# Turning x and the residual sum before they are normed, and squares summed on VectorE, in a one-core decoder trunk of two layers

## The reference

```
h = rms_norm(x, g)            # x * rsqrt(mean(x*x) + 1e-6) * g, over a row
# layer A: 16 heads of 64
q, k, v, gate = split(h @ w_in_a, 4)
x = x + (silu(gate) * stick_breaking(q, k, v)) @ w_out_a
# keys and values, shared: 8 heads, k = 2 components of 64, v = 128 wide
k, v = split(rms_norm(x, kv_norm_g) @ w_kv, 2)
k = rope(rms_norm(k, k_norm_g))
# layer B
q, gate = split(rms_norm(x, b_norm_g) @ w_in_b, 2)
q = rope(rms_norm(q, q_norm_g))
o = (softmax(q1 k1'/8) - lam * softmax(q2 k2'/8)) v       # causal
o = rms_norm(o, subln_g) * (1 - lam_init)
x = x + (silu(gate) * o) @ w_out_b
```

## Time and profile before

| | us |
|---|---|
| runs | 641.98, 640.73, 641.54 |
| median | 641.54 |
| profiled execution, its own time | 644.41 |
| span of that execution | 643.1 |
| TensorE busy | 620.0 (96%) |
| VectorE busy | 452.9 (70%) |
| ScalarE busy | 349.6 (54%) |
| GpSimd busy | 351.2 (55%) |
| chain that ended last, by engine | PE 65%, DVE 21%, ACT 7% |

### The profile page before, as it was taken

How to read it: one execution, slowest core, us unless ns; L and a number is a source line. 1 busy time by engine, 2 the same in 40 slices (tenths; PEclk the granted TensorE clock), 3 DMA queues, 4 the chain that set the end, 5 groups by cost and what they waited for, 6 DMA issues and landing times.

```text
span 643.1 us, 9970 instructions
## 1 busy us (share of the span) xinstructions
PE 620.0 (96%) x3260; PEld 522.0 (81%) x3260; DVE 452.9 (70%) x717; ACT 349.6 (54%) x764; POOL 351.2 (55%) x335
## 2 busy tenths in 40 slices
PE   5899999999999999999989999999899999999998
PEld 4788887888888888878878888788687888887786
DVE  3476168989889898884146398426789999998531
ACT  5342284967869678684336544325356645576320
POOL 4557448547576475735342545457564676556161
PEclk9999998999999999999999999999899999999999
DMA  7433313112121121212121322230421220221142
GB/s 261 104 97 95 93 35 99 49 51 65 45 86 49 49 65 49 82 34 66 66 66 43 106 93 88 82 107 25 123 74 50 82 82 12 70 83 65 34 133 97
DMA packets 61774, 49.09 MB, mean 76 GB/s; under 512 B 7728, under 2 KB 48816, under 8 KB 61744
## 3 DMA queue, kind: packets, MB, share of 16 engines
q1 hardware_dynamic: 58064, 48.25, 24.4%
q10 hardware_dynamic: 3680, 0.46, 0.5%
HBM read 44.50 MB, written 2.10 MB: 72 GB/s over the span
## 4 chain that ended last, share of the span: by engine, by line
PE 65%; DVE 21%; ACT 7%; issue 4%; DMA 1%; SPq 0%; DVEq 0%; POOL 0%; ACTq 0%
PE bank L607 17%; PE bank L609 17%; PE bank L608 17%; PE bank L730 4%; ACT pr L1366 4%; PE bank L744 3%; PE bank L706 3%; DVE small L1749 1%; DVE pr L1770 1%; DVE lo L1561 1%; DVE h_hi L1494 1%; DVE lo L1539 1%; DVE v L1446 1%; DVE at_lo L1804 1%; DMA xs<-in_x 1%
## 5 line engine op out<-in xcount | busy, mean ns | idle before, releaser
L484 POOL TENSOR_TENSOR w_lo<-w_raw,w_hi 128x512 fp32r<-128x512 f32 x64 | 87.0, 1367 | 123.6 <-ACT w_hi L1045 123.6
L496 POOL TENSOR_TENSOR w_lo<-w_raw,w_hi 128x512 fp32r<-128x512 f32 x96 | 139.0, 1448 | 7.7
L494 POOL CAST w_hi<-w_raw 128x512 fp32r<-128x512 f32 x96 | 74.6, 777 | 120.7 <-DVE pr L1770 38.2
L607 PE MATMUL bank<-h_hi,w_hi 128*128 128x512 f32 x320 | 129.4, 404 | 2.8 <-ACT q L1275 2.7
L607 PE MATMUL bank<-w_hi,h_hi 128*128 128x512 f32 x320 | 128.6, 402 | 2.9 <-DVE h_lo L1452 2.8
L609 PE MATMUL bank<-w_hi,h_lo 128*128 128x512 f32 x320 | 126.1, 394 | 0.0
L608 PE MATMUL bank<-w_lo,h_hi 128*128 128x512 f32 x320 | 125.8, 393 | 0.0
L609 PE MATMUL bank<-h_hi,w_lo 128*128 128x512 f32 x320 | 125.5, 392 | 0.0
L608 PE MATMUL bank<-h_lo,w_hi 128*128 128x512 f32 x320 | 125.2, 391 | 0.0
L1045 ACT ACTIVATE w_hi<-w_raw 128x512 fp32r<-128x512 f32 x64 | 39.6, 628 | 65.0 <-PE bank L609 64.9
L607 PEld LDWEIGHTS bank<-h_hi,w_hi 128*128 128x128 f32 x320 | 60.1, 188 | 17.2 <-issue 2.2
(11 more groups left out here) (183 smaller groups left out, 1202.2 us busy)
## 6 DMA issues: line engine op xcount, KB each, us to landing
w_raw<-in_a_w_in SPq DMA_DIRECT2D x64, 256.0 KB, 2.7
w_raw<-in_w_kv SPq DMA_DIRECT2D x32, 256.0 KB, 3.0
w_raw<-in_b_w_in SPq DMA_DIRECT2D x32, 256.0 KB, 2.8
w_raw<-in_a_w_out SPq DMA_DIRECT2D x16, 256.0 KB, 2.8
w_raw<-in_b_w_out SPq DMA_DIRECT2D x16, 256.0 KB, 3.0
xs<-in_x SPq DMA_DIRECT2D x4, 512.0 KB, 4.8
qrot<-qs SPq DMA_DIRECT2D x32, 64.0 KB, 2.0
out_x<-xs SPq DMA_DIRECT2D x8, 256.0 KB, 2.7
```

The costliest lines, as they stand in the source:

```text
L484: nc.gpsimd.tensor_tensor(w_lo[s][:, :], w_raw[s][:, :], w_hi[s][:, :].bitcast(F32), ALU.subtract).then_inc(s_w, 1)
L494: nc.gpsimd.tensor_copy(w_hi[s][:, :], w_raw[s][:, :]).then_inc(s_whi, 1)
L496: nc.gpsimd.tensor_tensor(w_lo[s][:, :], w_raw[s][:, :], w_hi[s][:, :].bitcast(F32), ALU.subtract).then_inc(s_w, 1)
L607: pe.matmul(o, ahi, bhi, start=start, stop=False, skip_group_check=True)
```

## The change

Four things are written differently.

1. **Start.** TensorE transposes x itself, each of its four row blocks as it lands, with 4, 8, 4 and 8 `keep_busy` matmuls between. ScalarE and VectorE split the transposed x with the gain but without the root, into h2; the values' product runs on that, and the root is applied when the values are copied out (`scale=rx`). For q, k and gates the transposed x is copied raw, the roots are transposed too (`turn_roots`, four transposes), multiplied in by VectorE (`query_scale`) and split into h1 (`query_hi`, `query_lo`). Nine small parameters come by SyncE's queue between slabs. The rotary tables are built in one orientation and turned by eight transposes (`turn_tables`).
2. **Between the layers.** The same with the new stream: no `keep_busy`; tiles 0 to 3 are transposed inside the output product after its k=1 (`turn_sum(0)`), tiles 4 to 7 after the third step of the key/value product, with four transposes of the roots. Keys and values are scaled by the root as they are copied out. Banks are given by tables (`TURN_BANK`, `KV_BANK`).
3. **A head of layer B.** The squares are no longer summed on TensorE: they are transposed into banks 1 and 3 (`turned_squares`, eight transposes), and VectorE adds them there (`turned_means`, two `tensor_reduce`). `scores_b` of the next head, whose first matmuls write those banks, waits for it (s_rq). The root's logarithm and exponential stand one head later on ScalarE (`head_root` in `gate_parts`), and `at_lo` ahead of the means on VectorE. ScalarE takes over `keep_hi`, the hi part of two of each head's slabs and of the values; the copy of q stands before the last exponentials. GpSimd waits for the q rotation (s_qct) and for the roots (s_rb) before its splits, and the cosine product of `q_rotate` waits for q_lo.
4. **Last head.** ScalarE does two output slabs and the root of head 6 before the gate's logarithm.

```diff
+
+            tr = pe.transpose(bank[4 + k % 4][:, cols(t * P, P)], xs[:, t, cols(k * P, P)], ident[:, :])
+            if t == TT - 1:
+                tr.then_inc(s_tp, 1)
+
+        def turn_roots(n, o):
+
+            pe.wait_ge(s_rx, n + 1)
...
+                tr = pe.transpose(o[:, cols(t * P, P)], rx[:, t:t + 1].to_broadcast([P, P]), ident[:, :])
+            tr.then_inc(s_rt, 1)
...
-        keep_busy(neg_one[:, :], BUSY_A)
-        turn_input(0, 4, 0, 0)
+        for t in range(TT):
+            pe.wait_ge(s_x[t], 16)
+            for k in range(4):
+                turn_input(k, t)
+            keep_busy(neg_one[:, :], BUSY_A[t])
...
+                if half == 0 and k < 3:
+                    pe.wait_ge(s_raw, k + 1)
+                    for t in range(TT):
+                        turn_input(k + 4, t)
+                if half == 0 and k == 3:
+                    pe.wait_ge(s_raw, 4)
+                    turn_roots(0, bank[7])
+                if half == 0 and k == 4:
+                    pe.wait_ge(s_rc, 1)
+                    for t in range(TT):
+                        turn_input(7, t)
...
+        def turn_sum(half, tiles=range(TT)):
+
+            for k in (half * TT + n for n in tiles):
+                for t in range(TT):
+                    pe.wait_ge(s_x2, half * TT + t + 1)
+                    tr = pe.transpose(bank[TURN_BANK[k]][:, cols(t * P, P)], xs[:, t, cols(k * P, P)], ident[:, :])
+                tr.then_inc(s_tp, 1)
+
         for k in range(KT):
             bulk_step(G_OUT + KT + k, TT, k, h2_hi, h2_lo, banks_of=OUT_BANK_A)
-
-
-        pe.wait_ge(s_x2, TT)
-        keep_busy(h2_hi[:, 0, :], BUSY_B)
-        turn_input(0, 4, 1, 0)
+            if k == 1:
+                turn_sum(0)
...
-        turn_after = {12: 0, 13: 1, 15: 2, 16: 3, 20: 4, 21: 5, 22: 6, 24: 7}
+        def kv_step(grp, k):
+
+
+            if k:
+                bulk_step(kv_slab(grp * KT + k), 4 * grp, k, h2_hi, h2_lo, banks_of=KV_BANK)
+                return
+            for t in range(TT):
+                if grp >= 2:
+                    pe.wait_ge(s_vk, V_BY_ACT + KV_PRIOR[4 * grp + t] + 1)
+                bulk_step(kv_slab(grp * KT), 4 * grp, 0, h2_hi, h2_lo, banks_of=KV_BANK, tiles=(t,))
...
+        def turned_squares(h, o):
+
+            pe.wait_ge(s_cm, h + 1)
+            pe.wait_ge(s_qq, h + 2)
+            for i in range(TT):
+                tr = pe.transpose(bank[1][:, cols(i * P, P)], qsq[:, cols(i * P, P)], ident[:, :])
+            if o is not None:
+                pe.wait_ge(s_oq, o + 1)
+                for i in range(TT):
+                    tr = pe.transpose(bank[3][:, cols(i * P, P)], osq[:, cols(i * P, P)], ident[:, :])
+            tr.then_inc(s_sum, 1)
...
+                if grp == 0 and k == 2:
+                    turn_roots(1, bank[3])
+                    turn_sum(1, range(3))
+                    pe.wait_ge(s_rc, 2)
+                    turn_sum(1, (3,))
...
+            if not first:
+                pe.wait_ge(s_rq, h + (R_HEAD - 1))
...
-                sums(h + 1, h - 1 if n_before else None)
+                turned_squares(h, h - 1 if n_before else None)
...
+            A(v32[:, n % TT, cols(n // TT * HALF, HALF)], bank[n % 6][:, :], ACT.Copy,
+              scale=rx[:, n % TT:n % TT + 1]).then_inc(s_vk, 1)
...
             if gate is not None:
-                gate_parts(h - 1, gate)
+                gate_parts(h - 1, gate, second)
             elif later is not None and h == KT - 1:
                 gate_copies(h, later, 2 * KT - 2)
+                slab_hi(H_OUT + 2)
+                slab_hi(H_OUT + 3)
...
+                    if q_used is not None:
+                        q_copy(h + 3, q_used)
                     gate_exp(h + KT)
...
+            if keep:
+                act.wait_ge(s_og, h + (KT - 1))
...
                 gate_exp(h + KT + 1)
-            c0, c1 = mean_cols(first, not q_next)
...
+            if slabs is not None:
+                slab_hi(H_BODY + 4, *slabs)
+                slab_hi(H_BODY + 5, *slabs)
             for b in range(3):
                 act.wait_ge(s_tr, h * 3 + (b + 1))
                 A(at_hi[:, cols(*BANKS[b])], bank[BANK_B[0, b]][:, 0:BANKS[b][1]], ACT.Copy).then_inc(s_ah, 1)
+            if not q_next:
+                head_root(h, False, True)
+            if not first and q_next:
+                act.wait_ge(s_pv, h + KT)
+                A(vb_hi[:, :, :], v32[:, :, bass.ds(h * P, P)], ACT.Copy).then_inc(s_vh, 1)
...
+        dve.wait_ge(s_tbt, 1)
+        TS(sg_q[:, :], bank[2][:, :], gq_s, None, ALU.mult).then_inc(s_tbc, 1)
+        dve.wait_ge(s_tbt, 2)
+        TS(cg_q[:, :], bank[3][:, :], gq_c, None, ALU.mult).then_inc(s_tbc, 1)
...
+            dve.wait_ge(s_qk, n + (2 * KT - 1))
             TTN(qc[:, :], q32[:, :], cg_q[:, :], ALU.mult).then_inc(s_qct, 1)
...
+        def turned_means(with_o):
+
+            st.link(V.tensor_reduce(means[:, 0:8], comps(bank[1][:, :]), AX.X, ALU.add))
+            if with_o:
+                st.link(V.tensor_reduce(means[:, 8:12], bank[3].rearrange("p (t d) -> p t d", d=P), AX.X, ALU.add))
+            ins = TS(means[:, 0:8], means[:, 0:8], DH * EPS, None, ALU.add)
+            if with_o:
+                ins = STT(out=means[:, 8:12], in0=means[:, 8:12], scalar=1.0 / P, op0=ALU.mult, in1=eps_sums,
                           op1=ALU.add)
             ins.then_inc(s_rq, 1)
...
-                keep_hi(h - 2, h + (KT - 1))
...
+                    TTN(at_lo[:, cols(*BANKS[b])], bank[BANK_B[0, b]][:, 0:BANKS[b][1]],
+                        at_hi[:, cols(*BANKS[b])].bitcast(F32), ALU.subtract).then_inc(s_al, 1)
+
+            weights_lo(0, 1, 2)
             dve.wait_ge(s_sum, h + 2)
-            mean_squares(c0, c1)
+            if q_next:
+                turned_means(n_before)
+            else:
+                mean_squares(c0, c1)
             root_newton(c0, c1, h + R_HEAD).then_inc(s_rb, 1)
             st.link(STT(out=eps_sums, in0=tiny[:, 16:24:2], scalar=EPS, op0=ALU.mult, in1=tiny[:, 16:24:2],
                         op1=ALU.mult))
-            for b in range(3):
-                dve.wait_ge(s_ah, h * 3 + (48 + b + 1))
-                TTN(at_lo[:, cols(*BANKS[b])], bank[BANK_B[0, b]][:, 0:BANKS[b][1]],
-                    at_hi[:, cols(*BANKS[b])].bitcast(F32), ALU.subtract).then_inc(s_al, 1)
-            if q_after:
-                q_rotate(h + 3)
```

More of the change, by code:

```diff
@@ L1377, in head @@
                     q_square(2)
[L1378 to L1379 removed]
+            if q_used is not None and first:
+                q_copy(3, q_used)
             if later is not None and h == KT - 2:
```

410 lines of the change are left out of this document (249 added, 161 removed).

## The result

Four runs of the changed kernel took 624.4, 626.5, 625.59 and 623.77 us, median **625.0**; the kernel before, run beside it, 641.13. The ratio is 0.9741 (95% interval 0.9716 to 0.9766): 16.1 us faster, as forecast (625.5). The sum came out closer than its terms did.

What follows compares the result with a forecast made beforehand. TensorE, busy 620.0 of 643.1 us, was taken to bound the kernel. Terms -6.25 - 5.64 - 7.2 + 3.1 = -16.0 from the 641.54 median gave 625.5 us; 8-in-10 range 616.5 to 632.5.

Steps and rivals of the forecast that it cites:

- Start: Layer A's start: first product at 12.65 instead of 19.95, less 1.05 us of added transposes: -6.25 us, bounds -9.2 and 0.
- the slow stretch: After the first product: TensorE at half speed for 5.97 us as before; up to 2.9 us more gained if shorter.
- Between the layers: Output product to key/value product: the 7.39 us gap goes, 1.75 of transposes come: -5.64 us, bounds -5.64 and about 0.
- Heads: Layer B heads 0 to 7: -0.50, -3.54 and five times -0.63, together -7.2 us; bounded by -11.7 without the new wait.
- their wait: First masks of a layer B head wait about 0.75 us for VectorE's reductions of the turned squares.
- the period: Distance of first masks in heads 2 to 7: 19.23 us instead of 19.86, five times -0.63, -3.15 us.
- The 0.38 for q's copy: Layer B heads: TensorE's wait for q's copy, 1.5 us in four heads, 0.38 a head, goes.
- head 1 to 2: Layer B, second head: 22.26 us becomes 18.72, without the 1.59 wait and 1.70 of low clock: -3.54 us.
- the clock fall: Layer B, second head: 3.40 us of work at granted clock 0.50, costing 1.70 us, goes.
- Last head: Layer B's last head: reductions and attend 1.4 us later, a clock fall of 1.7: +3.1 us, bounds 0 and +3.1.
- The rival of contention: Layer B: cosine product stays slow beside GpSimd, at_lo 1.06 us later in six heads: +6.4, 631.9 us; chance 0.15.

Runs made afterwards that it cites:

- second trace: The kernel before, unedited, profiled once more: span 638.8 us after 643.1 in its first profile; its runs took 640.0 us.
- first pair: The first profiles of the kernel before and of the changed kernel, no further edit: spans 643.1 and 623.2 us.
- Experiment 7: Changed kernel with the first sixteen transposes of the residual sum behind the output product's last step instead of its second: 632.16 us, ratio 0.9867.
- experiment 4: Changed kernel with head 6's root ahead of the two output slabs' copies on ScalarE in the last head: 625.51 us, ratio 0.9735.
- experiment 8: Changed kernel with GpSimd's layer B splits waiting for the combined probabilities again, not the cosine product and roots: 641.87 us, ratio 1.0045.
- experiment 3: Changed kernel with the squares summed on TensorE into bank 7 again, without turned squares or their reductions: 637.72 us, ratio 0.9937.

## Why the prediction was right, and where it was not

*Start*: forecast -6.25, measured -8.0 in one pair of traces and -5.1 in the other, the mean -6.5. The step that failed is the speed: I let the slow stretch last 5.97 us after the first product, as before. It lasted 0 or 2.7 us (and in the kernel before's second trace 3.6). The first product was 0.7 later than computed, since the second block of x landed after TensorE was done with the first. The two errors have opposite signs. Over the ten traces whose kernels have this start the pairs begin 6.6 us sooner than in the two of the kernel before.

*Between the layers*: forecast -5.64, measured -6.1 in both pairs. Experiment 7 confirms the mechanism, and adds that its price without that place includes the clock.

*Heads*: forecast -7.2, measured -7.0 by the first pair and -5.4 by the second. The chain at_hi, at_lo, reductions, masks and their wait (0.75 forecast, 0.5 to 0.7 measured) were right, the period 0.1 off. Three terms were mis-sized. The eight transposes of the squares take 0.87 us, not 0.70, so 0.83 goes with the sums, not 1.00, as the changed kernel's timeline shows:

```profile
496.40 0.60 PE L919 MATMUL bank<-ident,qsq 128*128 128x128 f32 x4
...
497.27 1.26 PE L990 MATMUL bank<-ident,pr 128*128 128x128 f32 x10
```

The 0.38 for q's copy rested on 1.5 us in four heads, of which 1.01 was one wait; the second trace has heads 2 to 7 19.52 apart, not 19.86. And head 1 to 2 came to 19.70, not 18.72: the clock fall went, as said, but the squares' transposes there wait 0.8 us for the combined probabilities, a wait that I had not priced. In the changed kernel's timeline:

```profile
458.12 0.66 PE L919 MATMUL bank<-ident,qsq 128*128 128x128 f32 x4 [0.81 <-DVE pr L1965]
```

*Last head*: forecast +3.1, measured +2.7. The size is right, the working isn't. I put the reductions 1.4 later, and they are 2.9 later: ScalarE's two copies cost 1.0 (experiment 4), the root and its steps ahead of the gate's 0.7, and GpSimd's split beside the gate's step 1.1, which the prediction did not see. Against that, attend is 2.3 later and the clock takes 1.7, yet the last stage is just 2.7 longer, so 1.3 us were taken up behind attend. Of these, 0.5 us is a wait of the kernel before that the changed one no longer has, the rest is open:

```profile
595.40 1.05 PE L843 MATMUL bank<-small,osq 128*128 128x1 f32 x8 [0.54 <-DVE ot L1736]
```

*The rival of contention* was right in kind and far too small. I counted one product, 1.06 a head, 6.4 in all. Without GpSimd's waits the price is 12 us by the profiled executions and 16.9 by the medians (experiment 8): it hits two or three VectorE instructions in each head, the wait at the masks becomes 2.5 in three of them, and the lower mean clock adds to it. The GPSIMD Engine Reference of the Trainium skill (Specifications) names two SBUF inputs as one of the cases of contention, and the traces agree: 1.28 against 0.16 for a step of four columns with two SBUF inputs, no lengthening of the one with one input beside it. But one input is no safeguard: in the kernel before, `keep_hi` (L1494), a cast of one SBUF tile, took 1.48 us beside a split and 0.41 where GpSimd did nothing:

```profile
576.75 1.48 DVE L1494 CAST h_hi<-og 128x512 fp32r<-128x512 f32 x1
...
595.27 0.41 DVE L1494 CAST h_hi<-og 128x512 fp32r<-128x512 f32 x1
```

The change moves it to ScalarE; what that alone is worth was not tried. What puzzled me, that `qs` with the same inputs was short in the earlier trace rows, is a matter of when: in the kernel before's head 4 `qs` starts at 523.44, ahead of the split at 523.59, and `qc` at 524.04 in the midst of it. The split ends at 525.28, `qc` 0.55 later.

So the total was right partly by luck. By the two pairs of traces the start gave 1.8 more or 1.2 less than forecast and the heads 0.2 or 1.8 less; the seam gave 0.5 more and the last head cost 0.4 less, and together they cancel.

## What to carry to other kernels

Price a VectorE instruction with two SBUF operands by what GpSimd is running when it is issued, up to the whole rest of that instruction; a four-column step can cost 1.1 us, and making GpSimd wait can be what a change lives from. Look at what stands just hidden behind the work that you remove (here `ot`, 0.8 us). Profile both kernels twice before a term below 2 us is believed, and compare by stage: two executions of these kernels agree to 0.15 us in the stages where neither the clock nor one wait differs. Count the clock's part before a cause is named: in experiment 3 it was 8.5 of 13.1 us.
